# A two-layer trunk on one core: outer products and attention of the second mixer as three products of rounded fp32

## What is computed

```python
DEPTH, D_MODEL, SEQ = 2, 1024, 512
def gla_mixer(h, w_in, w_gate_up, b_gate, g_norm, w_out):    # H = 4 heads, DK = 128, DV = 256
    q, k, v, z_lr, r = jnp.split(h @ w_in, splits, axis=-1)
    g = log_sigmoid(z_lr @ w_gate_up + b_gate) / 16.0
    ...
    def step(state, inp):
        ...
        attn = jnp.einsum('bhtk,bhsk,bhtsk->bhts', qj, kj, decay)
        o = jnp.einsum('bhts,bhsv->bhtv', attn, vj) + \
            jnp.einsum('bhtk,bhkv->bhtv', qj * jnp.exp(bj), state)
        state = state * jnp.exp(b_last)[..., None] + jnp.einsum('bhsk,bhsv->bhkv', k_dec, vj)
        return state, o
    ...
    o = rms_norm(o) * g_norm * silu(r)
    return o @ w_out
def reference(x, ...):
    h = x
    for i in range(DEPTH):       # i = 0: softmax attention of 16 heads; i = 1: gla_mixer
        h = h + mixer_i(rms_norm(h, norm_mix_g[i]))
        h = h + jnp.square(jax.nn.relu(rms_norm(h, norm_mlp_g[i]) @ mlp_w_up[i])) @ mlp_w_down[i]
    return rms_norm(h, norm_final_g)
```

## Time and profile before

| | |
|---|---|
| median of 3 runs | 1152.51 us (1152.2 to 1152.59) |
| the profiled execution | 1152.45 us, its span 1150.4 us |
| TensorE busy | 1140.1 us (99% of the span) |
| VectorE busy | 795.1 us (69%) |
| ScalarE busy | 564.2 us (49%) |
| GpSimd busy | 40.3 us (4%) |
| read from memory | 103.57 MB |

### The profile page before, as it was taken

One profiled execution on the slowest core, in us unless ns is written; L12 is line 12 of the kernel. 1 busy time (PEld: TensorE's weight loads), 2 busy tenths in 40 slices (PEclk: granted clock), 3 DMA queues, 4 the chain that ended last, 5 costly groups with the idle time before them and its releaser, 6 DMA issues.

```text
span 1150.4 us, 14690 instructions
## 1 busy us (share of the span) xinstructions
PE 1140.1 (99%) x5569; PEld 958.8 (83%) x5569; DVE 795.1 (69%) x1072; ACT 564.2 (49%) x793; POOL 40.3 (4%) x86
## 2 busy tenths in 40 slices
PE   8999999999999999999999999999999999999997
PEld 7788888888888888888878988998888888888886
DVE  5648888546865856948867775593578488487486
ACT  4447677436535435435556333253454364453454
POOL 1000000000000000000020101010000000000001
PEclk9999999999999999999999999999999999999999
DMA  9365756423062161251341330205113415215201
GB/s 287 71 133 120 149 127 165 141 98 110 1 225 69 40 216 36 73 183 37 111 139 48 111 97 14 74 19 165 61 49 108 148 37 167 89 36 182 93 31 76
DMA packets 115994, 119.07 MB, mean 103 GB/s; under 512 B 38754, under 2 KB 83842, under 8 KB 115940
## 3 DMA queue, kind: packets, MB, share of 16 engines
q1 hardware_dynamic: 113072, 117.26, 34.5%
q10 hardware_dynamic: 2868, 1.07, 0.4%
HBM read 103.57 MB, written 2.10 MB: 92 GB/s over the span
## 4 chain that ended last, share of the span: by engine, by line
PE 98%; DMA 1%; ACT 0%; DVE 0%; issue 0%; POOL 0%; SPq 0%; POOLq 0%; ACTq 0%; DVEq 0%
PE bank L1099 10%; PE bank L1102 10%; PE bank L1103 10%; PE bank L1264 9%; PE bank L1268 9%; PE bank L1269 9%; PE bank L1112 6%; PE bank L1116 6%; PE bank L1115 6%; PE bank L1368 3%; PE bank L1371 3%; PE bank L1372 3%; PE bank L1412 2%; PE bank L1399 2%; PE bank L1544 2%; PE bank L1486 1%
## 5 line engine op out<-in xcount | busy, mean ns | idle before, releaser
L660 ACT ACTIVATE w_hi<-w_stage 128x2048 fp32r<-128x2048 f32 x80 | 152.0, 1912 | 148.8 <-PE bank L1264 92.3
L1752 DVE TENSOR_TENSOR w_lo<-w_stage,w_hi 128x2048 fp32r<-128x2048 f32 x88 | 200.6, 2287 | 32.2 <-ACT w_hi L660 11.9
L1099 PE MATMUL bank<-hT_lo,w_hi 128*128 128x512 f32 x512 | 200.0, 391 | 0.0
L1103 PE MATMUL bank<-hT_hi,w_lo 128*128 128x512 f32 x512 | 199.5, 390 | 0.0
L1102 PE MATMUL bank<-hT_hi,w_hi 128*128 128x512 f32 x512 | 199.4, 390 | 0.0
L1264 PE MATMUL bank<-w_lo,u_hi 128*128 128x512 f32 x336 | 131.7, 392 | 0.0
L1269 PE MATMUL bank<-w_hi,u_lo 128*128 128x512 f32 x336 | 131.0, 390 | 0.0
L1268 PE MATMUL bank<-w_hi,u_hi 128*128 128x512 f32 x336 | 130.9, 390 | 0.0
L1099 PEld LDWEIGHTS bank<-hT_lo,w_hi 128*128 128x128 f32 x512 | 96.2, 188 | 20.6 <-DVE hT_lo L1826 0.5
L1103 PEld LDWEIGHTS bank<-hT_hi,w_lo 128*128 128x128 f32 x512 | 96.2, 188 | 20.0
L1102 PEld LDWEIGHTS bank<-hT_hi,w_hi 128*128 128x128 f32 x512 | 96.2, 188 | 19.4
(11 more groups left out here) (247 smaller groups left out, 2017.9 us busy)
## 6 DMA issues: line engine op xcount, KB each, us to landing
w_stage<-in_mlp_w_up_dram SPq DMA_DIRECT2D x32, 1024.0 KB, 5.5
w_stage<-in_mlp_w_down_dram SPq DMA_DIRECT2D x32, 1024.0 KB, 6.2
w_stage<-in_fox_w_in_dram SPq DMA_DIRECT2D x36, 256.0 KB, 5.1
w_stage<-in_gla_w_in_dram SPq DMA_DIRECT2D x8, 1024.0 KB, 5.4
qa<-qk_hi SPq DMA_DIRECT2D x32, 128.0 KB
keys<-qk_hi SPq DMA_DIRECT2D x16, 256.0 KB
w_stage<-in_fox_w_out_dram SPq DMA_DIRECT2D x4, 1024.0 KB, 5.3
w_stage<-in_gla_w_in_dram SPq DMA_DIRECT2D x8, 512.0 KB, 4.7
```

The source lines that it names most:

```text
L660: act.activation(w_hi[:, HI_SLOT[unit], :], w_stage[:, STAGE[unit], :], ACT.Copy).then_inc(w_hi_made, 1)
L1099: a = pe.matmul(out, w[0][:, k, :], x[1][:, k, :], start=(k == 0), stop=False)
L1103: a = pe.matmul(out, w[1][:, k, :], x[0][:, k, :], start=False, stop=(k == KT - 1))
L1752: dve.tensor_tensor(w_lo[:, to, :], w_stage[:, at, :], fp(w_hi[:, to, :]), ALU.subtract).then_inc(w_lo_made, 1)
```

## The change

`outer` and `attend` become three rounded products each. Their operands are split: `gv` and `tailT` are written rounded where they were written as fp32, and `since`, `state` and `attnT` get rounded copies by ScalarE; five residuals are made by VectorE. The new tiles lie over existing memory: `gv_lo` over the fourth slot of `w_stage` (so weights are staged in three slots during this mixer, and the last unit of the output weights is loaded only when `go_done` has reached 8), `since_hi` and `state_hi` over `ql` and `decay`, and the two parts of `attnT` over the tiles that hold the pairs of `level(a, 0)`. So the next head's `pairs`, `keep_pair` and first `decayed` wait until `attend` has read them. The lists of all three engines are reordered in the second mixer, and in the first mixer a head's projection is made in one piece ahead of `values`, for heads 0 to 11.

```diff
+def stage_of(c):
+    return (c - GLA_U) % (SLOTS - 1) if GLA_U <= c < GLA_OUT_U + 3 else slot_of(c)
...
+        gv_lo = over("gv_lo", [P, TB, 2 * DV], "w_stage", UNIT)
+        since_hi = over("since_hi", [P, TB - 1, P], "ql", S)
+        state_hi = over("state_hi", [P, TB - 1, DV], "decay", 2 * S)
...
-                    late = 1 if c in (GLA_U, GLA_U + 2) else 0
+                    late = 1 if c in (GLA_U, GLA_U + 2) or c >= GLA_U + SLOTS - 1 else 0
                     sp.wait_ge(w_lo_made, c - SLOTS + 1 + late)
+                    if c == GLA_OUT_U + 3:
+                        sp.wait_ge(go_done, 2 * GLA_H)
...
+                if a and lv == 0:
+                    act.wait_ge(go_done, 2 * a)
                 first, w = (S // 2, S // 2) if lv else (0, S)
                 act.activation(pair_hi[:, 0:w], decay[:, lv % 2, first:first + w], ACT.Copy).then_inc(pair_hi_made, 1)
+
+            def state_rounded(a):
+                act.wait_ge(state_made, (a + 1) * (TB - 1))
+                act.wait_ge(level_done, a * (LEVELS + 1) + LEVELS)
+                act.activation(state_hi[:], state[:], ACT.Copy).then_inc(state_hi_made, 1)
+
+            def attn_rounded(a):
+                act.wait_ge(level_kept, (a + 1) * (LEVELS + 1))
+                act.activation(attn_hi, attnT, ACT.Copy).then_inc(attn_hi_made, 1)
...
                 if head + 3 < FOX_H:
-                    project_qk(head + 3, range(KT // 2))
+                    project_qk(head + 3, range(KT if head < LAST_WHOLE else KT // 2))
...
                 for c in range(TB - 1):
-                    mm = pe.matmul(bank[2 + c // 2][:, (c % 2) * DV:(c % 2 + 1) * DV], tailT[:, c, :],
-                                   gv[:, c, a % 2 * DV:(a % 2 + 1) * DV], start=True, stop=True)
+                    to = bank[2 + c // 2][:, (c % 2) * DV:(c % 2 + 1) * DV]
+                    pe.matmul(to, tailT[:, c, :], gv_lo[:, c, part], start=True, stop=False)
+                    pe.matmul(to, tailT[:, c, :], gv[:, c, part], start=False, stop=False)
+                    mm = pe.matmul(to, tailT_lo[:, c, :], gv[:, c, part], start=False, stop=True)
...
+                mm.then_inc(states_used, 1)
+                pe.wait_ge(attn_lo_made, a + 1)
                 for c in range(TB):
-                    mm = pe.matmul(to[c], attnT[:, c, :], gv[:, c, a % 2 * DV:(a % 2 + 1) * DV], start=False, stop=True,
-                                   skip_group_check=True)
+                    pe.matmul(to[c], attn_hi[:, c, :], gv_lo[:, c, part], start=False, stop=False, skip_group_check=True)
+                    pe.matmul(to[c], attn_hi[:, c, :], gv[:, c, part], start=False, stop=False, skip_group_check=True)
+                    mm = pe.matmul(to[c], attn_lo[:, c, :], gv[:, c, part], start=False, stop=True, skip_group_check=True)
...
                 dve.wait_ge(gk_copied, a + 1)
                 if a:
                     dve.wait_ge(ql_made, a * SCALINGS)
+                    dve.wait_ge(states_used, a)
...
+            def v_residual(pair, t):
+                dve.wait_ge(gv_copied, pair * TB + t + 1)
+                dve.scalar_tensor_tensor(out=gv_lo[:, t, :], in0=bank[gv_bank(pair, t)][:], scalar=rstd[:, t:t + 1],
+                                         in1=fp(gv[:, t, :]), op0=ALU.mult, op1=ALU.subtract).then_inc(gv_lo_made, 1)
```

More of the change, by code:

```diff
@@ L136, in loaded @@
 def loaded(c, slot):
-    earlier = sum(loads_of(u) for u in range(c + 1) if plain(u) and slot_of(u) == slot)
+    earlier = sum(loads_of(u) for u in range(c + 1) if plain(u) and stage_of(u) == slot)
     return earlier + (c >= GLA_U) * GROUPS * LOADS_PER_SLOT[slot]
@@ L198, in fox_gla_trunk, with over @@
     with ExitStack() as ctx:
+        ends = {}
         def sb(name, shape, dt=F32, at=ctx):
-            return at.enter_context(nc.sbuf_tensor(name, shape, dt))
+            tile = at.enter_context(nc.sbuf_tensor(name, shape, dt))
+            ends[name] = nc.sbuf_base
+            return tile
+        def over(name, shape, last, count):
+            return nc.alloc_sbuf_tensor_at(name, shape, F32R, offset=ends[last] - 4 * count)
         def sem(name):
@@ L440, in load_rows @@
                 for j in range(4):
-                    load(i, per, c + j, *rows_of(src, row + (j % 2) * (KT // 2), (j // 2) * S, slot_of(c + j)))
+                    load(i, per, c + j, *rows_of(src, row + (j % 2) * (KT // 2), (j // 2) * S, stage_of(c + j)))
             def load_fox(c):
@@ L1563, in outer @@
                 mm.then_inc(kv_done, 1)
             def attend(a):
-                pe.wait_ge(qsince_made, a + 1)
+                part = slice(a % 2 * DV, (a % 2 + 1) * DV)
                 to = [bank[2 + c // 2][:, (c % 2) * DV:(c % 2 + 1) * DV] for c in range(TB)]
+                pe.wait_ge(since_lo_made, a + 1)
+                pe.wait_ge(state_lo_made, a + 1)
                 for c in range(1, TB):
-                    pe.wait_ge(state_made, a * (TB - 1) + min(c + 1, TB - 1))
-                    pe.matmul(to[c], since[:, c, :], state[:, c - 1, :], start=(c < 3), stop=False,
+                    pe.matmul(to[c], since_hi[:, c - 1, :], state_lo[:, c - 1, :], start=(c < 3), stop=False,
@@ L2249, in _ @@
             pairs_lo(1, 0)
+            decayed(1, 1)
+            differences(1, 2)
+            split_lo(0, 0, c + 6)
             outputs(0)
-            differences(1, 2)
-            decayed(1, 1)
             keep(1, 0)
             keep_through(1)
+            decayed(1, 2)
             differences(1, 3)
-            decayed(1, 2)
-            split_lo(0, 0, c + 7)
+            differences(1, 4)
             keep(1, 1)
-            differences(1, 4)
             decayed(1, 3)
             keep(1, 2)
+            decayed(1, 4)
             differences(1, 5)
-            decayed(1, 4)
+            differences(1, 6)
+            silus(1)
+            split_lo(0, 0, c + 7)
+            tail_residual(1)
             keep(1, 3)
-            silus(1)
-            split_lo(0, 0, c + 8)
-            differences(1, 6)
             decayed(1, 5)
             keep(1, 4)
+            decayed(1, 6)
             last_differences(1)
-            decayed(1, 6)
+            split_lo(0, 0, c + 8)
             keep(1, 5)
+            last_decayed(1)
             states(1)
-            split_lo(0, 0, c + 9)
-            last_decayed(1)
             pairs_lo(1, 7)
+            keep(1, 6)
+            since_residual(1)
+            state_residual(1)
+            keep(1, 7)
+            attn_residual(1)
             keep_qk(2)
-            keep(1, 6)
             pairs(2)
-            keep(1, 7)
             differences(2, 1)
@@ L2350, in _ @@
             keep(3, 6)
+            since_residual(3)
+            state_residual(3)
+            keep(3, 7)
+            attn_residual(3)
             split_lo(0, 0, c + 13)
-            keep(3, 7)
             split_lo(0, 0, c + 14)
```

229 lines of the change are left out of this document (148 added, 81 removed).

## The result

The changed kernel takes 1154.81 us (median of 15, 1153.32 to 1155.47) beside 1152.45 before: ratio 1.0018, 95% interval 1.0011 to 1.0024 (the medians alone give 1.0020), so about 0.2% slower. The forecast was 1152.3 us with a range of 1149.4 to 1154.7, and the median lies 0.1 us above it. The 15 times are no single cloud: seven lie at 1153.3 to 1154.0, eight at 1154.8 to 1155.5, with mean granted TensorE clocks of 0.999 in all seven and 0.997 to 0.998 in all eight. The median is thus the lowest of the upper group, the eight longer times; with one execution fewer in it, it would have been 1154.0, inside the range. The profiled execution, 1153.4 us, is one of the seven.

The account below looks back on a forecast made before the run. TensorE's own list was taken to bound the kernel (busy 1140.1 of 1150.4 us). Terms: -2.9 - 0.45 + 2.4 + 0.3 + 0.45 + 0.2 = 0.0 us; it took 1152.3 us, range 1149.4 to 1154.7.

Parts of the forecast that it names:

- The products: `outer`, state and attention parts, second mixer: 40 products replaced by three rounded ones each, -2.9 us, 0.72 in each head.
- no wait would come in heads 0 to 2: Second mixer: TensorE's inputs stay ready, smallest spares 1.3 us (second level of head 1) and 1.5 (`attend(1)`); taken as 0.
- Head 3, its start: Ahead of `project_gr(3, 0)`: TensorE waits from T + 3.17 for `silus` on VectorE at T + 5.5, +2.4 us, bounds 1.8 and 3.
- Head 3, its end: VectorE nearly gapless: +0.3 us at two transposes and the first output product, +0.45 at the attention part of `attend(3)`.
- the old wait: TensorE's present 0.37 us wait ahead of the first output product, with 0.1 of refill, is replaced: -0.45 us.
- The failed step: Last transposes: `squares(3)` comes behind two weight roundings, `outputs(3)` ends about T + 42.9, TensorE there at T + 42.7: +0.2 us.
- T: The end of `attend(2)` on TensorE, from which the prediction counts times in head 3.
- VectorE runs late in every head: Slower rival, chance 0.16: VectorE blocked by GpSimd's `since` products in heads 1 to 3, some 2.7 us reach TensorE: 1155.
- The first mixer: Projection in one piece ahead of `values`, transposes behind a short product: taken as 0, from -0.6 to +0.6 us for 12 heads.

Follow-up runs that it names:

- the run with full fp32: Changed kernel with `silus(2)` and `squares(3)`/`outputs(3)` moved earlier, each of 40 groups of three rounded products replaced by one full fp32 product: 1151.49 us.
- a gap of 4 us: Kernel before, with `silus(2)` put behind `decayed(3, 1)` on VectorE, nothing else: 1158.13 us, ratio 1.0052.
- the filled gap: Changed kernel with 20 unused products of 256 columns on TensorE ahead of `project_gr(3, 0)`: median 1153.69 us.
- the run with squares early: Changed kernel with `squares(3)` ahead of the second weight rounding on ScalarE and `outputs(3)` ahead of the second weight residual on VectorE: median 1151.67 us.
- the one with `silus` early: Changed kernel with first half of `silus(2)` right behind `pairs_lo(3, 0)` on VectorE and its `tanhs` ahead of `keep_pair(3, 0)` on ScalarE: 1151.31 us, ratio 0.9991.
- one of 6.7 us: Changed kernel with weight residual c + 12 put ahead of `silus(2)` on VectorE: median 1159.93 us.

## Why the prediction was wrong

**The products** were right in cost: 0.12 us a piece. In heads 0 to 2, where 2.16 us were forecast, 2.4 came (130.42 to 128.00 us), 2.2 of them by the products alone, as the run with full fp32 showed. That no wait would come in heads 0 to 2 was right too. In head 3 the 0.72 us of the sum save nothing.

**Head 3, its start** was right in place, releaser and size: +2.4 forecast, 2.6 by the starts in the two traces, and 3.5 us off the median when mended. What the step left out, and the sum with it, is what such a gap does to the clock: it put this at nothing, without a word. In eight of fifteen executions the time was 1.5 us more; filled, no execution had it; in the kernel before, a gap of 4 us brought a stretch at half clock in the trace. That the changed kernel's own upper group is this drop is inferred from the filled gap and the reported clocks, since no such execution was traced. The clocks alone are weak evidence: with three digits, 0.998 stands in both groups of the run with squares early, and in three of eleven executions of the one with `silus` early, which has one group.

**Head 3, its end**: forecast +0.3 and +0.45 for two transposes with the first output product, and `attend(3)`, and -0.45 for the old wait. The two timelines give about 0.4 and 0.4, and the old wait is gone.

**The failed step** is the one on `squares(3)`: "In the new order `outputs(3)` ends 4.3 us after the start of `squares`, about T + 42.9, and TensorE is there at T + 42.7: **+0.2**". The wait measured 1.7 us of idle time, and 1.9 us came off the trace and off the lower group when it was mended. With T = 738.1 the `squares` start at T + 39.2, `outputs(3)` ends at T + 45.3, 6.0 us behind them and not 4.3, and TensorE was there at T + 43.7. (The prediction doesn't show how it came to T + 42.7; by the terms of its own sum it would be T + 43.1.) The 4.3 us are what the kernel before needs, 776.15 to 780.42:

```profile
776.15 0.38 ACT L995 ACTIVATE o_all<-bank 128x256 f32<-128x256 f32 x1 [4.03 <-PE bank L1575]
777.07 0.19 POOL L544 TENSOR_TENSOR orstd<-oss,columns_of 128x2 f32<-128x2 f32 x1 [23.76 <-ACT o_all L995]
778.41 0.88 DVE L2191 SCALAR_TENSOR_TENSOR o_all<-bank,orstd,gb 128x256 f32<-128x256 f32 x2 [2.38 <-POOL orstd L623]
```

There VectorE is idle for 2.38 us while GpSimd works. In the new order it was in the middle of a long residual, and GpSimd, between `squares` and `outputs`, could not go on: 1.99 us instead of 0.19. The prediction had this pair of engines blocking each other only as a rival at another place (`since`, where VectorE is the one that waits), and in heads 0 to 2 no wait of TensorE came from it. The slower rival, "VectorE runs late in every head", was thus wrong in place and near in mechanism.

**The first mixer** was put at 0 with a bound of -0.6 and gave -0.3. In the twelve heads with the new order 0.05 us each are gone, as if the delay behind a short product were not paid when transposes follow, and half of that is lost again in the last heads.

**The sum** came to 0.0 us, and the prediction took 1152.3, 0.15 below the 1152.45 it started from, without a term for it. By the two traces: -0.4 ahead of the first mixer's heads, which is chance, -0.3 in them, -2.4 in heads 0 to 2, +2.6 and +1.7 in head 3 and behind it make +1.2 at the last product. With 1.5 us of clock in eight of fifteen executions the median is at +2.4. The range ended at 1154.7, 0.1 us too low, because its upper end priced late work of VectorE in every head, but neither the blocked GpSimd step nor the clock. That the median fell outside and not inside is chance: it hung on one execution.

## What to carry to other kernels

When work is added to an engine off the path, check one by one what stands *behind* the new waits in its list: here a half `silus` of 0.6 us, put behind seven more instructions of VectorE, cost 2.6 us, and moving it gave back 2.2 us of the lower group and 3.5 of the median. Before a short GpSimd step on the path, look at what VectorE is running at that moment: beside a 2.3 us instruction with two operands in memory a 0.2 us step lasted until that ended (1.99 and 1.47 us in two runs). Where a change leaves two groups of times, compare their granted clocks, and, since these can be too coarse to tell, try filling the gap with idle products: if the time falls, the gap costs more than its length.

## What the hardware showed that I had not expected

- Kernels with a gap of 2.4 us on TensorE in head 3 had some executions that were 1.4 to 1.7 us longer (8 of 15, 4 of 11, 6 of 11 in three kernels) and others that were not. With a gap of 1.7 us alone there was no second group in 11 executions. With one of 4.0 us and with one of 6.7 us there was one group of 5 each, at clocks of 0.995 to 0.998, and the one execution traced of each has a stretch at half clock.
- With the gap of 4.0 us the half clock began 1 us after work had started again (749.3 against 748.29) and lasted 3.4 us, so that the products that pay for it are not those next to the gap. With the gap of 6.7 us it began inside the gap.
- Behind a 128-column product the second of a run of 512-column products starts 0.05 us late; with transposes put between, a head's turn was 0.05 us shorter (9.10 for 9.15).
